# A twelfth ring unit for the experts' weights, laid over the context half of the residual stream

## The reference

```python
def moe_swiglu(h, w_router, w1, w3, w2):
    logits = (h @ w_router).astype(jnp.float32)
    top_logit, top_idx = lax.top_k(logits, TOP_K)          # 2 of 8
    gates = jax.nn.softmax(top_logit, axis=-1)
    ...
    def expert_block(args):
        xblk, e = args
        return (jax.nn.silu(xblk @ w1[e]) * (xblk @ w3[e])) @ w2[e]
```

## Time and profile before

| | us |
|---|---|
| median of three runs (2583.54 to 2587.51) | 2586.48 |
| the profiled execution | 2584.57 |
| its span, first to last instruction | 2582.8 |
| PE busy | 2492.0 (96%) |
| DVE busy | 1273.8 (49%) |
| ACT busy | 1004.2 (39%) |
| DMA, mean of 16 engines | 52.1% of the span on SP's queue |

### The profile page before, as it was taken

One profiled execution on the slowest core, in us unless ns is written; L12 is line 12 of the kernel. 1 busy time (PEld: TensorE's weight loads), 2 busy tenths in 40 slices (PEclk: granted clock), 3 DMA queues, 4 the chain that ended last, 5 costly groups with the idle time before them and its releaser, 6 DMA issues.

```text
span 2582.8 us, 44788 instructions
## 1 busy us (share of the span) xinstructions
PE 2492.0 (96%) x18590; PEld 1788.5 (69%) x18590; DVE 1273.8 (49%) x2273; ACT 1004.2 (39%) x1813; POOL 0.2 (0%) x4
## 2 busy tenths in 40 slices
PE   8999999999999999999999999999899999999897
PEld 6787777888788888886787789743466547843333
DVE  4877566334632223346866665623266528832122
ACT  5534366222522222236434564422255327622121
POOL 0000000000000000000000000000000000000000
PEclk8999999999999999999999999999999999999998
DMA  7011174222322223220011546699976899999996
GB/s 301 2 52 34 61 250 176 93 94 97 155 98 98 98 98 131 98 89 26 3 52 66 182 147 246 245 421 421 420 264 219 316 410 421 383 416 421 421 421 253
DMA packets 73549, 529.32 MB, mean 205 GB/s; under 512 B 8064, under 2 KB 9472, under 8 KB 9472
## 3 DMA queue, kind: packets, MB, share of 16 engines
q1 hardware_dynamic: 73056, 524.67, 52.1%
q10 hardware_dynamic: 288, 1.74, 0.2%
HBM read 525.33 MB, written 1.05 MB: 204 GB/s over the span
## 4 chain that ended last, share of the span: by engine, by line
PE 83%; DMA 8%; DVE 5%; ACT 3%; issue 1%; DVEq 0%; SPq 0%; ACTq 0%
PE bank L622 79%; DMA spare_units<-wstream 4%; DMA arena<-wstream 2%; PE bank L883 2%; ACT arena L1768 1%; PE bank L1304 1%; DMA layers_unit<-wstream 1%; DMA ring<-wstream 1%; DVE arena L2879 1%; PE bank L734 0%; DVE weights_low L2567 0%; ACT weights_high L1768 0%; PE bank L1089 0%; ACT hT L1768 0%; PE bank L1626 0%
## 5 line engine op out<-in xcount | busy, mean ns | idle before, releaser
L1768 ACT ACTIVATE arena<-bank 128x512 f32<-128x512 f32 (+6 forms) x564 | 266.6, 488 | 815.6 <-PE bank L622 740.7
L2567 DVE TENSOR_TENSOR weights_low<-ring,weights_high 128x1024 fp32r<-128x1024 f32 x220 | 266.8, 1224 | 398.7 <-ACT weights_high L1768 398.7
L1768 ACT ACTIVATE weights_high<-ring 128x1024 fp32r<-128x1024 f32 (+1 forms) x240 | 267.5, 1126 | 244.6 <-PE bank L622 222.5
L622 PE MATMUL bank<-h_low,weights_high 128*128 128x512 f32 (+1 forms) x960 | 347.9, 362 | 0.0
L622 PE MATMUL bank<-arena 64*64 64x64 f32 (+5 forms) x4944 | 267.6, 242 | 16.0 <-DVE arena L2782 4.5
L622 PEld LDWEIGHTS bank<-arena 64*64 64x64 f32 (+3 forms) x4944 | 224.4, 143 | 40.1 <-issue 14.5
L622 PEld LDWEIGHTS bank<-h_low,weights_high 128*128 128x128 f32 x960 | 182.3, 190 | 27.6
L622 PE MATMUL bank<-h_high_gates,weights_high 128*128 128x512 f32 (+1 forms) x512 | 174.3, 341 | 4.3 <-DVE weights_low L2567 3.6
L622 PE MATMUL bank<-h_high_ffn,weights_high 128*128 128x512 f32 x448 | 175.6, 392 | 0.8 <-ACT modT L1768 0.5
L622 PE MATMUL bank<-h_high_ffn,weights_low 128*128 128x512 f32 x448 | 174.8, 390 | 0.0
L622 PE MATMUL bank<-h_high_gates,weights_low 128*128 128x512 f32 (+1 forms) x512 | 173.0, 338 | 0.0
(11 more groups left out here) (417 smaller groups left out, 4474.2 us busy)
## 6 DMA issues: line engine op xcount, KB each, us to landing
ring<-wstream SPq DMA_DIRECT2D x271, 1024.0 KB, 5.0
arena<-wstream SPq DMA_DIRECT2D x99, 1024.0 KB, 12.9
spare_units<-wstream SPq DMA_DIRECT2D x62, 1024.0 KB, 13.4
layers_unit<-wstream SPq DMA_DIRECT2D x31, 1024.0 KB, 13.8
tables_unit<-wstream SPq DMA_DIRECT2D x31, 1024.0 KB, 14.2
xT<-xin SPq DMA_DIRECT2D x2, 1024.0 KB, 6.0
cn<-consts SPq DMA_DIRECT2D x1, 1595.5 KB, 22.2
sm<-small SPq DMA_DIRECT2D x1, 1568.0 KB, 25.5
```

The source lines that it names most:

```text
L622: return nc.tensor.matmul(o, lhsT, rhs, start=first, stop=last)
L1768: return nc.scalar.activation(o, i, func, **kw)
L2567: step(vx.tensor_tensor(ring_low[:, u % RING, cols], ring[:, u % RING, cols], wh[:, j % 4, :].bitcast(F32), ALU.subtract), "weights low", j)
```

## The change

The ring of the experts' part gets a twelfth slot, and the early slots a fifth. The new slot, `context_unit`, lies over the context columns of `xT`: eight pieces of 256 float32, 1 KB each, 2 KB apart in a partition. `pieces` shapes the source, or the buffer of the high part, like the slot; `columns` picks the same columns from either shape. The ring's lag becomes 12. The early slots start 14 dense units before the end of the dense stream, where they started 12 before it, again three units apart.

```diff
-MOE_RING = 11
+MOE_RING = 12
-EARLY_SLOTS = 4
+EARLY_SLOTS = 5
...
+        xT_at = nc.sbuf_base
         xT = sb("xT", [P, KD, TOK])
...
+        context_unit = nc.alloc_sbuf_tensor_at("context_unit", [P, KD, TOK], F32, offset=xT_at)
+        context_low = part("context_low", [P, KD, TOK], xT_at)
...
             if s < EARLY_SLOTS:
                 return ((spare_units[:, 0, :], spare_low[:, 0, :]), (spare_units[:, 1, :], spare_low[:, 1, :]),
-                        (layers_unit[:, :], layers_low[:, :]), (tables_unit[:, :], tables_low[:, :]))[s]
+                        (layers_unit[:, :], layers_low[:, :]), (tables_unit[:, :], tables_low[:, :]),
+                        (context_unit[:, :, 0:CTX], context_low[:, :, 0:CTX]))[s]
...
+        def pieces(view, like):
+
+            return view.rearrange("p (k c) -> p k c", k=KD) if len(like.shape) == 3 else view
+
+        def columns(view, cols):
+
+            return view[:, cols.start // CTX:cols.stop // CTX, :] if len(view.shape) == 3 else view[:, cols]
...
-            early_slots = {DENSE_UNITS - 3 * EARLY_SLOTS + 3 * s: s for s in range(EARLY_SLOTS)}
+            early_slots = {DENSE_UNITS - 14 + 3 * s: s for s in range(EARLY_SLOTS)}
...
-                    sp.dma_start(moe_slot(i, q)[0], wstream[first + q]).then_inc(unit_landed(i, q)[0], 16)
+                    sp.dma_start(moe_slot(i, q)[0], pieces(wstream[first + q], moe_slot(i, q)[0])).then_inc(unit_landed(i, q)[0], 16)
...
-                        ins = mm(o, left, moe_slot(i, q)[0][:, cols], first, last)
+                        ins = mm(o, left, columns(moe_slot(i, q)[0], cols), first, last)
...
-                        ins = mm(o, left[0], low[:, cols], False, last)
+                        ins = mm(o, left[0], columns(low, cols), False, last)
...
-                    f(moe_high(q), moe_slot(i, q)[0], ACT.Copy).then_inc(*tick(e_scalars, kind, "high", q))
+                    f(pieces(moe_high(q), moe_slot(i, q)[0]), moe_slot(i, q)[0], ACT.Copy).then_inc(*tick(e_scalars, kind, "high", q))
...
-                return vx.tensor_tensor(low, raw, moe_high(q).bitcast(F32), ALU.subtract)
+                return vx.tensor_tensor(low, raw, pieces(moe_high(q), raw).bitcast(F32), ALU.subtract)
```

More of the change, by code:

```diff
@@ L572, in _ @@
                     sp.wait_ge(*done("branch product", 1, 3))
-                    sp.dma_start(moe_slot(0, s)[0], wstream[DENSE_UNITS + s]).then_inc(moe_loaded[s], 16)
+                    sp.dma_start(moe_slot(0, s)[0], pieces(wstream[DENSE_UNITS + s], moe_slot(0, s)[0])).then_inc(moe_loaded[s], 16)
                 sp.wait_ge(unit_used, u - RING + 1)
@@ L611, in _ @@
                         sp.wait_ge(moe_used, j * MOE_UNITS + ((EXPERTS + 1) * MOE_UNITS + q - AGAIN_RING + 1))
-                        sp.dma_start(moe_slot(j, q)[0], wstream[first + q]).then_inc(again_loaded[q % AGAIN_RING], 16)
+                        sp.dma_start(moe_slot(j, q)[0], pieces(wstream[first + q], moe_slot(j, q)[0])).then_inc(again_loaded[q % AGAIN_RING], 16)
             for k in (0, KD // 2):
@@ L1523, in more_gate_up @@
                 for k in range(4):
-                    ins = mm(more_bank(p)[quarter(k), :], x2[:, 4 * b + k, :], moe_slot(LARGEST, q)[0][:, k * TOK:(k + 1) * TOK],
+                    ins = mm(more_bank(p)[quarter(k), :], x2[:, 4 * b + k, :], columns(moe_slot(LARGEST, q)[0], slice(k * TOK, (k + 1) * TOK)),
                              b == 0, b == 1)
@@ L1533, in more_down @@
                         ins = mm(bank[1][quarter(2 * n + c), :], gh2[:, 2 * q + c, :],
-                                 moe_slot(LARGEST, 2 * PAIRS + q)[0][:, c * D + n * 512:c * D + n * 512 + 512], q == 0, q == PAIRS - 1)
+                                 columns(moe_slot(LARGEST, 2 * PAIRS + q)[0], slice(c * D + n * 512, c * D + n * 512 + 512)), q == 0, q == PAIRS - 1)
                 ins.then_inc(*tick(more_products, "more spent", 2 * PAIRS + q))
@@ L2277, in next_high @@
                         act.wait_ge(*here("spent", MOE_UNITS + q - AHEAD))
-                    f(moe_high(q), moe_slot(i + 1, q)[0], ACT.Copy).then_inc(*tick(e_scalars, kind, "next high", q))
+                    f(pieces(moe_high(q), moe_slot(i + 1, q)[0]), moe_slot(i + 1, q)[0], ACT.Copy).then_inc(*tick(e_scalars, kind, "next high", q))
                 def keep_hidden(p):
```

## The result

| | before | after |
|---|---|---|
| median, us (19 runs each) | 2585.88 | 2590.08 |
| lowest to highest | 2582.15 to 2591.19 | 2584.04 to 2597.13 |
| the profiled execution | 2584.57 | 2588.03 |
| its span | 2582.8 | 2586.2 |

The ratio is 1.0015, with a 95% interval of 1.0009 to 1.0022: by it the change costs 3.9 us (2.3 to 5.7). The forecast was 2586.4, that is, no change against the median; the time lies inside the range of 2581.0 to 2591.5, but the sign was missed.

A forecast was written before the change was run, and what follows sets the result against it. DMA was taken to bound the experts' part up to 1852.52 us and again at the end, PE between. Slot gain -4.98 plus 15 x 0.45 gave +1.8 us on the profiled 2584.57: 2586.4 us, range 2581.0 to 2591.5.

The forecast's parts named there:

- the two switches: Where PE-bound work gives way to DMA-bound, at 1661.69 us and after the wide passes: each gains one transfer, 2.49 us.
- stages A, B and C: Experts' part: A DMA-bound up to 1852.52 us, B PE-bound to 2378.81 by the chain, C DMA-bound to the end, 2556.5.
- the 4.98 of the sum: Most the twelfth slot could gain in the experts' part: 2 x 2.49 us, one transfer at each start of DMA-bound work.
- Where the price lies: Of 28 units in pieces, only 6 in the first DMA-bound stage and 9 in the last cost time; others are covered.
- the second rival: Pieces cost as the output's stores do, 0.65 to 0.75 us each, full stretches at some 411 GB/s: +5.8 us; chance 0.15.
- The price's size: A unit in pieces on the DMA-bound path costs 0.45 us more, from a short stretch of 1 KB loads; bounds 0 and 0.72.
- +1.8: Whole kernel, in us: -4.98 for the slot plus 15 units in pieces at 0.45, added to the profiled 2584.57.
- The break-even price: Cost of one unit in pieces at which the slot's gain is used up: 4.98 / 15 = 0.33 us.
- 5.2 us: About 0.2% of the kernel's time, taken as what a measurement of it can tell from no change.
- What else moves: Earlier early transfers in the merge cost nothing (8 us to spare); PE, DVE and ACT read slots with gaps at no cost.
- That pieces cost nothing: Rival: units in pieces cost 0 to 0.1 us each, so the full -4.98 or 2579.6 us; chance 0.15.
- That stage A gains nothing: Rival: wide pass 2's start hangs on PE's end of pass 1, not a landing unit: +1.6 us, 2586.2; chance 0.1.

The follow-up runs named there:

- Twelve whole slots: Ring of 12 with the residual stream laid out so the twelfth slot is one 8 KB run, against the kernel before: 2578.45 us (0.9969), on another chip 2581.21 us (0.9984).
- the eleven slots with pieces: Ring of 11 as in the kernel before, but the slot over the tables replaced by one in eight 1 KB pieces: 2594.05 us, ratio 1.0029.
- two kernels of one set: Twelve whole rows, and the same with the twelfth slot's unit brought in 1 KB runs by two transfers: 2581.21 us and 2589.62 us.

## Why the prediction was wrong

**What bounds the kernel, and the two switches: right.** Full slices, stages A, B and C and their ends stand in the profile after where they stood before. Twelve whole slots gained 4.1 and 8.0 us and ten lost 7.5, beside the 4.98 of the sum; the 5.0 is within all three intervals. "At most" was too strong: in stage A the traces give the slot 2.7 to 3.4 us where one transfer is 2.49, and why it is more stays open.

**Where the price lies: right.** Fifteen units on the path, in packets of loads, and none in stage B. The rates fell by 1.4 to 1.7%, and the bytes of the full stretch by 1.8%, where 1.5 was named; the rates stayed above the 411 of the second rival.

**The price's size: the step that failed.** "I take **0.45**", with the remark that it is "rather too high than too low", was too low: the runs show 0.55 (bytes of a full stretch), 0.47 to 0.55 (length of A), 0.53 to 0.78 (length of C) and 0.56 (the medians of two kernels of one set); only the eleven slots with pieces come near it, at 0.44 (0.28 to 0.61). At 0.55 the sum is +3.3 in place of +1.8. By stage, A came out as forecast (0.1 us longer, 0.2 forecast) and C did not (3.1 longer, 1.6 forecast); why the lengths of C give the pieces a higher price than its bytes do stays open. The row for the price was a stretch of 0.34 us and 50 packets, in which the share was only 0.41; dividing by such a share assumes that busy time grows with the bytes. The break-even price was 0.33, so 0.1 us on one unit was worth 1.5 us on the whole.

**What it was added to: the second half of the miss.** The sum, +1.8, was put on one profiled execution, 2584.57, which lies 1.3 us below the median of the 19 runs. So "+1.8" came out as "equal to the median", although the working itself said slower. A sum of changes is better added to the median. Nor is 5.2 us the least that runs can tell from no change: the interval here, 2.3 to 5.7 us, leaves out zero. Of the 3.7 us between forecast and median the base is 1.3 and the price some 1.5; the rest lies within that interval.

**What else moves: right.** The early transfers cost nothing that shows (0.9998, 0.9989 to 1.0007): in the changed kernel SP passes at once from the end of a dense issue, 1533.48 + 6.08 = 1539.56, to the first early one at 1539.61, and DVE had begun on the fourth product at 1531.41.

```profile
1533.48 6.08 SPq L589 DMA_DIRECT2D ring<-wstream  x2
1539.61 0.43 SPq L585 DMA_DIRECT2D spare_units<-wstream  x1
```

The splits of pieces take what whole rows take; the changed kernel's instructions on the new slot and, in the second fence, on the slot next to it (least/median/most ns):

```profile
L634 PE MATMUL bank<-context_unit,tokens x96: 592/592/643, 1670.3 to 2514.1; 128*64 128x512 f32 x96
...
L615 SPq DMA_DIRECT2D context_unit<-wstream x27: 550/559/1999, 1672.3 to 2516.0; - x27
...
L1780 ACT ACTIVATE weights_high<-context_unit x8: 1910/1917/1925, 1868.5 to 2253.3; 128x2048 fp32r<-128x2048 f32 x8
L2976 DVE TENSOR_TENSOR context_low<-context_unit,weights_high x8: 2290/2292/2294, 1871.1 to 2255.2; 128x2048 fp32r<-128x2048 f32 x8
```

```profile
L634 PE MATMUL bank<-tables_unit,tokens x112: 592/592/644, 1667.3 to 2511.1; 128*64 128x512 f32 x112
...
L615 SPq DMA_DIRECT2D tables_unit<-wstream x27: 328/333/2051, 1669.3 to 2513.8; - x27
...
L1780 ACT ACTIVATE weights_high<-tables_unit x8: 1901/1917/1920, 1863.4 to 2250.6; 128x2048 fp32r<-128x2048 f32 x8
L2976 DVE TENSOR_TENSOR tables_low<-tables_unit,weights_high x8: 2286/2293/2294, 1867.2 to 2252.5; 128x2048 fp32r<-128x2048 f32 x8
```

**The rivals.** That pieces cost nothing is refuted by the rate of 413 GB/s with the engines as busy as before. That they cost as the stores do (0.65 to 0.75) is refuted by the bytes (0.55) and by stage A (0.47 to 0.55), though the truth lies about halfway between it and the forecast, and the lengths of C alone would allow it. That stage A gains nothing is refuted by the stage itself: at least 2.7 us less with whole rows, in two traces.

## What to carry to other kernels

One more slot in a ring is worth about one transfer for each switch from a stage that PE bounds to one that DMA bounds (here 2.2 to 4.0 us beside a transfer of 2.49), if the lead is kept until transfers lag. Spare memory in pieces costs a fixed time for each packet in a stage that DMA bounds, here some 10 ns on each engine, and little or nothing in one that PE bounds, so work out the price at which the slot breaks even, and change the layout so that the slot is one run before filling gaps. A gain of two transfers in 2.6 ms is near what runs can tell apart: read the price from the rate of a full stretch, and add the sum to the median.

## What was not expected of the hardware

SP takes 559 ns to issue a unit in pieces and 333 for one in whole rows (the rows above). It is not the number of packets that makes this: with four and with two pieces a unit takes 559 as well. Then SP is held: in the changed kernel's chain one issue to `ring` lasts from 2366.42 for 17.39 us, and those behind it follow at once, 0.33 us each.

```profile
2366.42 17.39 SPq L615
...
2384.00 0.33 SPq L615
...
2384.53 0.33 SPq L615
```

The timeline of SP shows the same four issues:

```profile
2366.42 18.97 SPq L615 DMA_DIRECT2D ring<-wstream  x4
```

In the kernel before such a group took 7.51 us at the same place.

```profile
2365.01 7.51 SPq L603 DMA_DIRECT2D ring<-wstream  x4
```

The longest single issue to `ring` grows with the packets of a unit on the new slot: 4.0 us with twelve whole slots (128 packets; 1.5 in stage C of before), 6.2 with two pieces (256), 10.5 with four (512) and 20.5 with eight (1024). That fits SP waiting for room in its queue, where a unit in pieces takes up to eight times as many packets; the queue itself is in no trace, so the reason is not shown. DMA's engines stay full meanwhile (share 1.02), so it costs nothing that the profile shows. It does change how the chain reads: it names SP for 28.9% of the stretch from 2280 to 2560 us, while the engines of DMA are the bound.

The clock is the other thing. The first matmuls on the third unit of wide pass 2, from the timeline of PE, in the first trace of before and in the first of the changed kernel (start, length of eight; in brackets the idle time before them and what ended it):

```profile
1858.25 1.93 PE L622 MATMUL bank<-arena,more_tokens 128*32 128x512 f32 x8 [2.57 <-DVE y_rows_low L3362]
```

```profile
1861.09 1.06 PE L634 MATMUL bank<-layers_unit,more_tokens 128*32 128x512 f32 x8 [2.58 <-DVE y_rows_low L3374]
```

PE had stood idle for as long in both; the eight matmuls took 1.93 us in the one and 1.06 in the other, beside granted clocks of 0.83 and 1.00. The idle time alone doesn't decide it, and what does stays open.
